# Sample state and memory rows loaded early into other buffers, their products spread over the inversion, half of the memory values' product inside cross attention

## Chip, cores and metric

One core of one Trainium2 chip. The time is that of one execution of the whole program on the device, in microseconds (us).

## What is computed

One decoder layer for a prompt of 256 tokens and 8 sample tokens that share the weights (model width 1024, 264 tokens in all):

```
x += W_out [ ConformerConv(group A) | GatedDeltaNet(group B) ](RMSNorm(x) @ W_in)
x += CrossAttn(RMSNorm(x), memory K/V)
x += MoE_top4of32_clampedSwiGLU(RMSNorm(x))
then a final RMSNorm

prompt, delta rule in chunks:  t_inv = (I + lower)^-1;  u = t_inv @ v_beta;  w = t_inv @ (k_beta * exp(gc))
                               v_new = u - w @ s;  o = (q * exp(g)) @ s + a @ v_new;  s = s * exp(g_last) + k' @ v_new
sample, delta rule in one step: s = s * exp(g);  v = (v - s.k) * beta;  s = s + k v^T;  o = s.q
memory:                        m = RMSNorm(mem);  mk = m @ w_mk;  mv = m @ w_mv      (prompt; kept as outputs)
cross attention:               softmax(q k^T / 16) v, with mk, mv for the prompt, a cache of K and V for each sample
```

The new states, the memory keys and values and the last rows ahead of both convolutions are outputs too. The state of the samples is 8 x 4 matrices of 128x128 (2 MB), each sample's cached keys and values are 256 x 1024 (1 MB each).

## The kernel before

The program has two parts. The second is the expert loop: 32 experts, whose weights (six pieces of 2 MB each) SP streams into eight slots, each piece being requested when TensorE has used the one before it in its slot. The first part, about 400 us, is everything up to the routing, and it is what the change touches.

In the first part TensorE's work is a list of jobs, `pre_moe_jobs`. Job n writes PSUM bank n modulo 8. It waits until job n-8 has been drained (copied out by VectorE or ScalarE), and for its operands. The list alone sets TensorE's order. VectorE and ScalarE each have an order of their own: over the inversion they walk through the same list and take what is theirs, after it their order is written out by hand. SP issues the loads of weights, states and caches in one written order, with waits for the release of each buffer; a wait there holds everything behind it. GpSimd issues the stores in the same way, and the broadcast of the sample queries.

The jobs that the text speaks of, in the order of the list before:

- `qkv`, `z`, `glu_b`, `glu_a`: projections (line L549), 3.6 us each. VectorE runs the short convolution on qkv, ScalarE its nonlinearity.
- The inversion, seven levels by doubling, two chunks: `inv_t` transposes (L698), `inv_x` multiplies (L705, copied by ScalarE), `inv_d` multiplies (L713, merged by VectorE at L1689). Between them stand fills, `glu_b` and `glu_a` in levels 1 to 4, `v_tok`, `k_tok` and `qk` in level 5, `z` 3 in level 6.
- `w_neg` (L722), `v_new` (L734), `state` (L744), `o_t` (L754): the products of the two chunks, each of which needs the copy of the one before it.
- `tail_g` (L850) and `tail_c` (L858): transposes for the rows kept as outputs; `s_decay`, `s_kq`, `s_krow`: small products for the samples.
- `s_read` (L782): each sample's state times its key and query; `s_rd` (L793) picks its diagonal blocks, `s_vrow` transposes the new values, and `s_outer` (L801) makes the outer products that VectorE adds into the state (L1741).
- `mem_t` (L809): transposes of the memory rows, copied by ScalarE; `mk`, `mv` (L819): memory keys and values, four jobs of 7 us each; `mk_t` (L829).
- `ln_mean`, `ln_var` (L569): need the whole wide convolution. That is 140 steps on VectorE (`conv_some`, L1628 to L1643, mostly L1630), done a few at a time between other work and the rest after `s_outer`.
- `w_out`, `q_s` (L885), `x_norm`, `xq`: to the queries. The sample queries go through memory and come back broadcast (`q_bc`, L519); VectorE multiplies them with each sample's cached keys (L1782), which frees the key's buffer (`k_used`).
- `s_score_t` (L925), `score` (L897), `prob_t` (L906), `s_prob_t`, `s_attn` (L945: cached values, freed by `v_used`), `attn` (L918), `s_attn_t`, `xo`, and the routing.

The buffers that matter: `ring` has twelve slots of 1 MB. Its first eight hold the weights (a group of 512 columns takes two), the last four (`scratch`) hold the inversion's tiles and the sample state, later cached keys and values. `region_m` holds the prompt's tiles, later the memory's. `region_p` holds the projections, later queries and probabilities. The loads around the change are on SP:

```
if g >= 4:
    wait_filled(sp, *LAST[g - 4])
sp.dma_start(wslot(g), cols(w, c0)).then_inc(sem(f"group{g % 4}"), 16)
if g == 8:
    wait_drained(sp, "inv_d", LEVELS - 1, 1)
    sp.dma_start(s_state, st_gdn[0].rearrange("b h k v -> k (b h) v")).then_inc(sem("s_state_in"), 16)
    wait_drained(sp, "state", 1)
    wait_drained(sp, "o_t", 1)
    sp.dma_start(mem_tok, mem_prompt[0].rearrange("(t p) d -> p t d", p=P)).then_inc(sem("mem_in"), 16)
```

## Time and profile before

| what | value |
|---|---|
| median of three runs | 1346.7 us (1345.5 to 1347.29) |
| the profiled execution | 1345.48 us, its span 1343.4 us |
| mean granted TensorE clock | 0.988 |
| TensorE (PE) busy | 1297.1 us, 97% |
| VectorE (DVE) busy | 456.9 us, 34% |
| ScalarE (ACT) busy | 222.4 us, 17% |
| GpSimd (POOL) busy | 28.8 us, 2% |
| bytes moved | 469.98 MB, mean 350 GB/s |
| expert loop | from 400.10 us on |

The shares are means over parts that differ: the expert loop takes 70% of the span and has TensorE and the DMA engines busy all the time. A line of the timeline gives start, duration, engine, line of the kernel, operation, tiles and count; idle time of the engine ahead of it stands in brackets with what ended it. A float32 matmul shows as two records.

### The profile page before, as it was taken

How to read it: one execution, taken by the hardware profiler on the slowest of the kernel's cores; microseconds unless marked ns; L12 is line 12 of the kernel's file. 1: busy time of each engine (PE TensorE's matmuls, PEld its weight loads, DVE VectorE, ACT ScalarE, POOL GpSimd, SP SyncE). 2: the span in 40 equal slices, each digit the busy share in tenths (PEclk: the TensorE clock that was granted, in tenths of full speed). 3: DMA queues.
4: the chain of work that ended last, by engine and by line, in shares of the span. 5: the costliest groups of instructions: out<-in, count | busy, mean ns of one | idle time of the engine just before them, and what ended most of it. 6: DMA issues, size and time to landing. Idle time of an engine off the chain costs nothing.

```text
span 1343.4 us, 17566 instructions
## 1 busy us (share of the span) xinstructions
PE 1297.1 (97%) x6598; PEld 610.5 (45%) x6598; DVE 456.9 (34%) x1324; ACT 222.4 (17%) x454; POOL 28.8 (2%) x73
## 2 busy tenths in 40 slices
PE   9999779998999999999999999999999999999996
PEld 6878754686663333333333333333333333333333
DVE  4655739218332222322223322223322223322224
ACT  3241132321131001101001101001110001110002
POOL 3000010000000000000000000000000000000000
PEclk9999889998999999999999999999999999999998
DMA  9310166498867999999999999999999999999992
GB/s 310 143 64 0 56 239 213 162 349 342 312 279 304 425 428 428 428 429 428 428 429 428 429 428 428 429 428 429 429 427 429 429 429 428 428 429 428 429 428 83
DMA packets 56651, 469.98 MB, mean 350 GB/s; under 512 B 6852, under 2 KB 7077, under 8 KB 32029
## 3 DMA queue, kind: packets, MB, share of 16 engines
q1 hardware_dynamic: 50538, 457.34, 82.1%
q0 software_dynamic: 3264, 11.40, 2.5%
q10 hardware_dynamic: 2819, 0.83, 0.3%
q8 instruction: 20, 0.33, 0.1%
q14 instruction: 10, 0.08, 0.0%
HBM read 463.84 MB, written 6.29 MB: 350 GB/s over the span
## 4 chain that ended last, share of the span: by engine, by line
PE 86%; DMA 7%; DVE 4%; ACT 1%; issue 1%; DVEq 0%; SPq 0%; POOL 0%; POOLq 0%; ACTq 0%
PE bank L1006 53%; PE bank L549 10%; PE bank L1052 5%; DMA ring<-in_w_gu 5%; PE bank L819 4%; PE bank L1019 3%; PE bank L1038 2%; PE bank L1032 1%; DMA region_p<-q_scratch 1%; PE bank L705 1%; PE bank L897 1%; PE bank L713 1%; PE bank L625 1%; DVE ring L1782 1%; PE bank L945 1%
## 5 line engine op out<-in xcount | busy, mean ns | idle before, releaser
L1006 PE MATMUL bank<-ring,region_p 128*64 128x512 f32 x2304 | 503.1, 594 | 1.7 <-DMA ring<-in_w_gu 1.0
L1006 PEld LDWEIGHTS bank<-ring,region_p 128*64 128x64 f32 x2304 | 163.0, 137 | 325.7 <-issue 321.8
L1937 DVE TENSOR_SCALAR region_p<-bank 128x512 f32<-128x512 f32 x32 | 22.1, 692 | 613.4 <-PE bank L1038 613.4
L1006 PE MATMUL bank<-region_m,region_p 128*64 128x512 f32 x768 | 169.5, 594 | 0.5 <-DMA region_m<-in_w_gu 0.5
L549 PE MATMUL bank<-hT,ring 128*128 128x264 f32 x512 | 119.6, 391 | 0.0
L1914 DVE TENSOR_TENSOR xT<-xT,bank 128x264 f32<-128x264 f32 x264 | 95.3, 423 | 60.7 <-PE bank L1052 60.7
L549 PEld LDWEIGHTS bank<-hT,ring 128*128 128x128 f32 x512 | 96.5, 192 | 16.1 <-issue 0.4
L1006 PEld LDWEIGHTS bank<-region_m,region_p 128*64 128x64 f32 x768 | 54.3, 137 | 108.7 <-issue 107.3
L1006 PE MATMUL bank<-region_p 128*64 128x512 f32 (+1 forms) x396 | 97.1, 608 | 0.1
L1393 ACT COPY region_p<-bank 128x264 f32<-128x264 f32 x33 | 12.5, 378 | 473.4 <-PE bank L1032 473.4
L1052 PE MATMUL bank<-region_p 64*128 64x264 f32 x528 | 81.0, 415 | 0.5 <-ACT region_p L1393 0.5
L1415 ACT COPY region_p<-bank 128x512 f32<-128x512 f32 x32 | 18.7, 585 | 244.8 <-PE bank L1006 244.8
L1052 PEld LDWEIGHTS bank<-region_p 64*128 64x128 f32 x528 | 49.5, 186 | 15.9 <-DVE xT L1914 5.9
L819 PE MATMUL bank<-ring,region_m 128*128 128x512 f32 x128 | 56.0, 594 | 0.3 <-DVE ring L1741 0.3
L1630 DVE SCALAR_TENSOR_TENSOR region_p<-region_p,par 128x256 f32<-128x256 f32 x120 | 48.3, 476 | 0.0
L1019 PEld LDWEIGHTS bank<-ident,region_p 128*128 128x128 f32 x260 | 27.2, 141 | 38.6 <-DVE region_p L1945 26.0
L1006 PEld LDWEIGHTS bank<-region_p 128*64 128x64 f32 (+1 forms) x396 | 22.4, 134 | 47.3 <-issue 45.6
L1019 PE MATMUL bank<-ident,region_p 128*128 128x128 f32 x260 | 42.6, 287 | 0.7 <-ACT region_p L1397 0.7
L819 PEld LDWEIGHTS bank<-ring,region_m 128*128 128x128 f32 x128 | 24.1, 190 | 29.4 <-issue 27.8
L1038 PE MATMUL bank<-region_p 32*64 32x512 f32 x384 | 35.2, 613 | 0.0
L1945 DVE TENSOR_TENSOR region_p<-region_p 128x512 f32<-128x512 f32 x32 | 33.6, 1051 | 1.1
L1397 ACT COPY region_p<-bank 128x512 f32<-128x512 f32 x33 | 19.3, 585 | 65.9 <-PE bank L1006 65.9
(378 smaller groups left out, 903.1 us busy)
## 6 DMA issues: line engine op xcount, KB each, us to landing
ring<-in_w_gu SPq DMA_DIRECT2D x96, 2048.0 KB, 20.7
ring<-in_w_dn SPq DMA_DIRECT2D x48, 2048.0 KB, 24.7
region_m<-in_w_gu SPq DMA_DIRECT2D x32, 2048.0 KB, 22.1
region_m<-in_w_dn SPq DMA_DIRECT2D x16, 2048.0 KB, 26.1
ring<-in_w_in SPq DMA_DIRECT2D x6, 2048.0 KB, 15.6
ring<-in_cache_mem_k SPq DMA_DIRECT2D x6, 1024.0 KB, 15.3
ring<-in_cache_mem_v SPq DMA_DIRECT2D x6, 1024.0 KB, 9.8
ring<-in_w_mk SPq DMA_DIRECT2D x2, 2048.0 KB, 8.4
```

The source lines that it names most:

```text
L549: m = pe.matmul(ps(key)[:, 0:width], w[:, k, f * P:(f + 1) * P], src[:, k, 0:width], start=(k == 0), stop=(k == KT - 1))
L819: ins = pe.matmul(ps(key)[:, :], memT[:, k, t * P:(t + 1) * P], wslot(g)[:, k, :], start=(k == 0), stop=(k == KT - 1))
L1006: ins = pe.matmul(bank[n][u * SLOTS:(u + 1) * SLOTS, :], lhs, rhs, start=start, stop=stop)
L1019: ins = pe.transpose(bank[dst_bank][:, c * P:(c + 1) * P], n[:, c * P:(c + 1) * P], ident[:, :])
L1038: ins = pe.matmul(bank[n][u * SLOTS:(u + 1) * SLOTS, :], one_hot[r * E:(r + 1) * E, :], bias_sb[r * E:(r + 1) * E, u * 512:(u + 1) * 512], ...
L1052: pe.matmul(bank[SCATTER_BANKS[n % 4]][:, 0:T], y_rows[u * SLOTS:(u + 1) * SLOTS, c * P:(c + 1) * P], scat[u * SLOTS:(u + 1) * SLOTS, :], ...
L1397: act.copy(hg_rows, bank[2][:, :]).then_inc(sem("hg_rows_ready"), 1)
L1415: act.copy(y_rows, bank[5][:, :]).then_inc(sem("y_ready"), 1)
L1630: ins = dve.scalar_tensor_tensor(out=conv[:, f, 0:TP], in0=src, scalar=dw(j, f), in1=conv[:, f, 0:TP], op0=ALU.mult, op1=ALU.add)
L1914: dve.tensor_tensor(xT[:, d, :], xT[:, d, :], bank[SCATTER_BANKS[n % 4]][:, 0:T], ALU.add).then_inc(sem("scat_added"), 1)
L1937: dve.tensor_scalar(xg, bank[0][:, :], 7.0, None, ALU.min).then_inc(sem("glu_clipped"), 1)
L1945: dve.tensor_tensor(act_rows.rearrange("p (v q) -> p q v", v=4), xl.rearrange("p (q v) -> p q v", v=4), sg.rearrange("p (q v) -> p q v", v ...
```

## The change

The list of jobs is written anew. `tail_g` moves up between the projections. `v_tok`, `qk` and `k_tok` become fills of levels 1 to 4, `z` 3 and the small sample jobs fills of level 5, `s_read` a fill of level 6. The memory's transposes stand between the state products. `s_outer` follows directly on `mk` 0. `mv` 0 and 1 stand beside `ln_mean` and `ln_var`, `mv` 2 and 3 go behind `score` in cross attention, on both sides of `s_score_t`. The attn jobs are split around both halves of `s_attn`.

The sample state is loaded in two halves, into `region_p` (free after the short convolution) and into `scratch` (free after `qk`), the memory rows into `region_p` after `k_tok`. All three loads stand on SP ahead of group 7. The weights of `mv` 2 and 3 become group 13, behind those of `w_out` and `xq`. Cached keys and values have five buffers instead of six. VectorE's convolution steps are spread anew over the levels: 81 of 140 stand ahead of `s_outer` instead of 78. ScalarE waits for the state's store ahead of the copies of `xq`. GpSimd's store of the memory values moves behind the broadcasts. VectorE takes the sample scores after the prompt's, and sums `s_attn_t` by four reductions instead of sixteen small operations.

```
-    fill = [[(n, i)] for i in range(4) for n in ("glu_b", "glu_a")]
-    fill += [[("v_tok", 0), ("v_tok", 1), ("k_tok", 0), ("k_tok", 1)], [("qk", 0), ("qk", 1)], [("z", 3)]]
+    turned = [[], [("v_tok", 0), ("v_tok", 1)], [("qk", 0), ("qk", 1)], [("k_tok", 0)], [("k_tok", 1)], [], []]
+    solved = [[]] + [[("glu_b", i)] for i in range(4)] + [[("z", 3)], [("s_read", 0), ("s_read", 1)]]
+    merged = [[]] + [[("glu_a", i)] for i in range(4)] + [[("tail_c",), ("s_krow",), ("s_decay",), ("s_kq",)]]
...
+    jobs += [("mem_t", 6), ("mem_t", 7), ("mk", 0)]
     jobs += [("s_outer", g) for g in range(sample_groups)]
-    jobs += [("mk", 2), ("mk", 3)]
...
+    jobs += [("mv", 2), ("s_score_t",), ("mv", 3)]
...
-        jobs += [("s_prob_t",)] if t == 0 else [("s_attn", 0)]
-    jobs += [("attn", d) for d in range(8)] + [("s_attn", 1), ("s_attn_t",)]
+    jobs += [("s_prob_t",)] + [("attn", d) for d in range(4)] + [("s_attn", 0), ("attn", 4), ("attn", 5)]
+    jobs += [("s_attn", 1), ("attn", 6), ("attn", 7), ("s_attn_t",)]
...
-        s_state = carve(scratch, 0, BH * P, "p (c n) -> p c n", c=BH)
+        s_state = [carve(base, 0, BH * P // 2, "p (c n) -> p c n", c=BH // 2) for base in (region_p, scratch)]
...
-              for v in [ring[:, 8 + i, :] for i in range(4)] + [region_m[:, 0:2048], region_m[:, 4096:6144]]]
+              for v in [ring[:, 8 + i, :] for i in range(4)] + [region_m[:, 4096:6144]]]
...
+                if g == 7:
+                    for j in range(3):
+                        wait_filled(sp, "tail_g", j)
+                    sp.wait_ge(sem("qkv_conv"), QF)
+                    half = st_gdn[0].rearrange("(m b) h k v -> m k (b h) v", m=2)
+                    sp.dma_start(s_state[0], half[0]).then_inc(sem("s_state_in"), 16)
+                    for c in range(NT):
+                        wait_drained(sp, "qk", c)
+                    sp.dma_start(s_state[1], half[1]).then_inc(sem("s_state_in"), 16)
+                    wait_drained(sp, "k_tok", 1)
+                    sp.dma_start(mem_tok, mem_prompt[0].rearrange("(t p) d -> p t d", p=P)).then_inc(sem("mem_in"), 16)
                 if g >= 4:
                     wait_filled(sp, *LAST[g - 4])
                 sp.dma_start(wslot(g), cols(w, c0)).then_inc(sem(f"group{g % 4}"), 16)
...
-                        conv_some(10)
+                        conv_some({2: 10, 3: 10, 4: 13, 5: 13}[lv])
...
-                        conv_some(6)
+                        conv_some(7)
...
+            act.wait_ge(sem("s_state_out"), 32)
```

**TensorE, levels 5 and 6 and the state products.** Before, from the fifth inv_x on (`ring 128x128` is inv_x, the first L549 z 3):

```order
L705 MATMUL bank<-ring 128x128 x8
L678 MATMUL bank<-ident,region_p 128x128 x16
L713 MATMUL bank<-region_m,ring 128x128 x8
L688 MATMUL bank<-region_p 128x128 x8
L698 MATMUL bank<-ident,region_m 128x128 x8
L705 MATMUL bank<-ring 128x128 x8
L549 MATMUL bank<-hT,ring 128x264 x8
L713 MATMUL bank<-region_m,ring 128x128 x8
L722 MATMUL bank<-region_m 128x128 x4
```

The same place now (L710 is inv_x, L718 inv_d, L864 tail_c, L703 inv_t, L787 s_read, L798 s_rd, L727 w_neg):

```order
L710 MATMUL bank<-ring 128x128 x8
L554 MATMUL bank<-hT,ring 128x264 x8
L718 MATMUL bank<-region_m,ring 128x128 x8
L864 MATMUL bank<-ident,region_p 38x128 x4
L776 MATMUL bank<-ident,rn 128x128
L767 MATMUL bank<-small,ones 128x64
L771 MATMUL bank<-small,ones 128x32
L703 MATMUL bank<-ident,region_m 128x128 x8
L710 MATMUL bank<-ring 128x128 x8
L787 MATMUL bank<-region_p,rn 32x512 x4
L787 MATMUL bank<-ring,rn 32x512 x4
L718 MATMUL bank<-region_m,ring 128x128 x8
```

The sixteen transposes of v_tok and k_tok (L678) and qk (L688) are gone from level 5, and s_read stands where z 3 stood.

**TensorE in cross attention.** Before (L925 is s_score_t, L897 score, L906 prob_t, L931 s_prob_t, L945 s_attn, L918 attn):

```order
L925 MATMUL bank<-ident,s_sc 32x128 x2
L897 MATMUL bank<-region_m,region_p 128x256 x16
L906 MATMUL bank<-ident,region_p 128x128 x8
L931 MATMUL bank<-ident,mix 128x32 x2
L906 MATMUL bank<-ident,region_p 128x128 x8
L945 MATMUL bank<-ring,mix 32x512 x8
L945 MATMUL bank<-region_m,mix 32x512 x8
L918 MATMUL bank<-region_p,region_m 128x256 x16
L945 MATMUL bank<-ring,mix 32x512 x16
```

Now (L824 is mv):

```order
L903 MATMUL bank<-region_m,region_p 128x256 x16
L824 MATMUL bank<-ring,region_m 128x512 x8
L931 MATMUL bank<-ident,s_sc 32x128 x2
L824 MATMUL bank<-ring,region_m 128x512 x8
L912 MATMUL bank<-ident,region_p 128x128 x16
L937 MATMUL bank<-ident,mix 128x32 x2
L924 MATMUL bank<-region_p,region_m 128x256 x8
L951 MATMUL bank<-ring,mix 32x512 x4
L951 MATMUL bank<-region_m,mix 32x512 x4
L951 MATMUL bank<-ring,mix 32x512 x8
L924 MATMUL bank<-region_p,region_m 128x256 x4
L951 MATMUL bank<-ring,mix 32x512 x8
```

The prompt's scores come first, two mv jobs stand behind them, and four matmuls (two attn jobs) remain between the halves of s_attn instead of sixteen.

## Rows read from the trace of the kernel before

**Rows 1.** The page, span in 40 slices of 33.6 us, tenths: granted clock, DMA share

```profile
PEclk9999889998999999999999999999999999999998
DMA  9310166498867999999999999999999999999992
```

**Rows 2.** Windows of 20 us: busy us (and instructions) per engine, clock, DMA share, GB/s

```profile
140.00:160.00 20.00, 15.06 (x99) 13.88 (x98) 17.62 (x39) 2.34 (x4) 0.00 (x0) 0.83 0.00 1
...
180.00:200.00 20.00, 16.30 (x68) 8.98 (x69) 5.40 (x17) 7.76 (x17) 1.01 (x2) 0.76 0.53 195
...
220.00:240.00 20.00, 18.82 (x56) 9.35 (x55) 20.00 (x52) 6.32 (x13) 0.72 (x1) 1.00 0.76 240
...
320.00:340.00 20.00, 13.20 (x60) 9.93 (x64) 12.85 (x66) 7.70 (x22) 0.00 (x0) 0.83 0.63 252
```

**Rows 3.** Timeline of TensorE, inversion to s_read: start, us, idle before in brackets

```profile
92.57 3.73 PE L549 MATMUL bank<-hT,ring 128*128 128x264 f32 x16
...
102.95 2.02 PE L705 MATMUL bank<-ring 128*128 128x128 f32 x16 [0.44 <-DVE ring L1683]
...
148.45 1.25 PE L698 MATMUL bank<-ident,region_m 128*128 128x128 f32 x8 [1.43 <-DVE region_m L1689]
153.21 3.76 PE L705 MATMUL bank<-ring 128*128 128x128 f32 x16 [3.51 <-DVE ring L1683]
156.76 4.68 PE L549 MATMUL bank<-hT,ring 128*128 128x264 f32 x16
...
164.25 1.13 PE L722 MATMUL bank<-region_m 128*128 128x128 f32 x8 [1.02 <-DVE region_m L1689]
...
183.69 3.64 PE L782 MATMUL bank<-ring,rn 128*32 128x512 f32 x16 [6.45 <-issue]
```

**Rows 4.** Timeline of TensorE: first mk job, ln_mean, w_out

```profile
191.80 7.11 PE L819 MATMUL bank<-ring,region_m 128*128 128x512 f32 x16
...
240.67 1.95 PE L569 MATMUL bank<-region_p,ones 128*128 128x264 f32 x8
...
257.97 28.64 PE L549 MATMUL bank<-mix,ring 128*128 128x264 f32 x128
```

**Rows 5.** DMA: us from issue to landing; cache loads (L392); the second q_bc

```profile
ring<-in_state_gdn SPq DMA_DIRECT2D x1, 0.5 KB, 19.5
```

```profile
DMA to landing us min/median/max: 6.4/10.6/20.4
```

```profile
304.98 8.02 DMA region_p<-q_scratch
```

**Rows 6.** Timeline of TensorE in cross attention, and the expert loop's first matmuls

```profile
324.43 0.59 PE L925 MATMUL bank<-ident,s_sc 128*32 128x128 f32 x2 [4.86 <-DVE s_sc L1782]
324.88 9.36 PE L897 MATMUL bank<-region_m,region_p 128*128 128x256 f32 x32
336.09 1.35 PE L906 MATMUL bank<-ident,region_p 128*128 128x128 f32 x8 [1.86 <-DVE region_p L1808]
...
342.89 7.17 PE L918 MATMUL bank<-region_p,region_m 128*128 128x256 f32 x32
349.99 3.64 PE L945 MATMUL bank<-ring,mix 128*32 128x512 f32 x32
...
400.10 2.94 PE L1006 MATMUL bank<-region_p 128*64 128x512 f32 x12
```

**Rows 7.** Timeline of VectorE: inv_t copies, s_outer to the convolution's end

```profile
152.38 1.28 DVE L1683 COPY ring<-bank 128x512 f32<-128x512 f32 x2
...
206.98 8.36 DVE L1741 SCALAR_TENSOR_TENSOR ring<-ring,small,bank 128x128 f32<-128x128 f32 x32 [3.06 <-PE bank L801]
215.26 21.46 DVE L1630 SCALAR_TENSOR_TENSOR region_p<-region_p,par 128x256 f32<-128x256 f32 x54
...
238.80 1.32 DVE L1748 SCALAR_TENSOR_TENSOR mix<-mix,par 128x1056 f32<-128x1056 f32 x1
```

More of the change, by code:

```diff
@@ L24, in pre_moe_jobs @@
         jobs += [("qkv", f), ("x_t", f - 1)]
-    jobs += [("qkv", f) for f in range(9, 12)]
-    jobs += [("z", 0), ("decay_small",)]
+        if f == 6:
+            jobs += [("tail_g", 0)]
+    jobs += [("qkv", 9), ("qkv", 10), ("tail_g", 1), ("qkv", 11)]
+    jobs += [("z", 0), ("tail_g", 2), ("decay_small",)]
     jobs += [("decay_row", 0), ("decay_row", 1), ("beta_row", 0), ("beta_row", 1)]
@@ L33, in pre_moe_jobs @@
     for lv in range(1, levels):
-        jobs += [("inv_x", lv, 0), ("inv_x", lv, 1)]
-        jobs += fill.pop(0)
-        jobs += [("inv_d", lv, 0), ("inv_d", lv, 1)]
+        jobs += turned[lv] + [("inv_x", lv, 0), ("inv_x", lv, 1)]
+        jobs += solved[lv] + [("inv_d", lv, 0), ("inv_d", lv, 1)]
         if lv < levels - 1:
-            jobs += fill.pop(0)
-            jobs += [("inv_t", lv, 0), ("inv_t", lv, 1)]
-    for f in fill:
-        jobs += f
-    jobs += [("w_neg",), ("v_new", 0), ("state", 0), ("v_new", 1), ("o_t", 0), ("o_t", 1), ("state", 1)]
@@ L43, in pre_moe_jobs @@
-    jobs += [("tail_g", j) for j in range(3)] + [("tail_c",)]
-    jobs += [("s_decay",), ("s_kq",), ("s_krow",), ("s_read", 0), ("s_read", 1)] + [("mem_t", c) for c in range(8)]
-    jobs += [("s_rd",), ("mk", 0), ("s_vrow",), ("mk", 1)]
+            jobs += merged[lv] + [("inv_t", lv, 0), ("inv_t", lv, 1)]
+    jobs += [("s_rd",), ("w_neg",), ("v_new", 0), ("mem_t", 0), ("mem_t", 1), ("state", 0), ("o_t", 0), ("s_vrow",)]
+    jobs += [("mem_t", 2), ("mem_t", 3), ("v_new", 1), ("mem_t", 4), ("mem_t", 5), ("state", 1), ("o_t", 1)]
@@ L46, in pre_moe_jobs @@
+    jobs += [("mem_t", 6), ("mem_t", 7), ("mk", 0)]
     jobs += [("s_outer", g) for g in range(sample_groups)]
-    jobs += [("mk", 2), ("mk", 3)]
-    jobs += [("o_norm", h) for h in range(4)]
-    jobs += [("mv", 0), ("mv", 1)] + [("mk_t", j) for j in range(4)]
-    jobs += [("ln_mean",), ("mv", 2), ("ln_var",), ("mv", 3)]
+    jobs += [("mk", 1), ("mk", 2), ("mk", 3)]
+    jobs += [("o_norm", h) for h in range(4)] + [("mk_t", j) for j in range(4)]
+    jobs += [("ln_mean",), ("mv", 0), ("ln_var",), ("mv", 1)]
@@ L1250, in _ @@
             order = sorted(JOB, key=JOB.get)
-            for key in order[JOB[("inv_t", 0, 0)]:JOB[("w_neg",)]]:
+            for key in order[JOB[("inv_t", 0, 0)]:JOB[("mk", 0)]]:
                 if key[0] == "inv_x":
@@ L1270, in _ @@
-            wait_filled(act, "tail_c")
-            drained(act.copy(tail_rows[0:HC + TS, :], ps(("tail_c",))[0:HC + TS, :]), ("tail_c",))
-            ln_exp_table()
-            wait_filled(act, "s_decay")
-            act.activation(s_eg, ps(("s_decay",))[:, 0:BH], ACT.Exp)
-            drained(act.copy(s_beta, ps(("s_decay",))[:, BH:2 * BH]), ("s_decay",))
-            wait_filled(act, "s_krow")
-            drained(act.copy(k_row, ps(("s_krow",))[:, 0:P]), ("s_krow",))
-            for m in range(2):
-                wait_filled(act, "s_read", m)
-                drained(act.copy(s_prod[m], ps(("s_read", m))[:, :]), ("s_read", m))
@@ L1281, in _ @@
[L1281 to L1283 removed]
+                elif key[0] == "tail_c":
+                    wait_filled(act, "tail_c")
+                    drained(act.copy(tail_rows[0:HC + TS, :], ps(("tail_c",))[0:HC + TS, :]), ("tail_c",))
+                elif key[0] == "s_krow":
+                    wait_filled(act, "s_krow")
+                    drained(act.copy(k_row, ps(("s_krow",))[:, 0:P]), ("s_krow",))
+                elif key[0] == "s_decay":
+                    ln_exp_table()
+                    wait_filled(act, "s_decay")
+                    act.activation(s_eg, ps(("s_decay",))[:, 0:BH], ACT.Exp)
+                    drained(act.copy(s_beta, ps(("s_decay",))[:, BH:2 * BH]), ("s_decay",))
+                elif key[0] == "s_read":
+                    m = key[1]
+                    wait_filled(act, "s_read", m)
+                    drained(act.copy(s_prod[m], ps(("s_read", m))[:, :]), ("s_read", m))
+                elif key[0] == "w_neg":
+                    wait_filled(act, "w_neg")
+                    drained(act.mul(w_neg.rearrange("p h n -> p (h n)"), ps(("w_neg",))[:, :], -1.0), ("w_neg",))
+                elif key[0] == "v_new":
+                    c = key[1]
+                    wait_filled(act, "v_new", c)
+                    drained(act.copy(v_new[c].rearrange("p h n -> p (h n)"), ps(("v_new", c))[:, :]), ("v_new", c))
+                elif key[0] == "mem_t":
+                    c = key[1]
+                    wait_filled(act, "mem_t", c)
+                    drained(act.mul(memT[:, c, :], ps(("mem_t", c))[:, 0:NMEM], pcol("mem", c)), ("mem_t", c))
```

174 lines of the change are left out of this document (86 added, 88 removed).

## The prediction

> **What bounds the kernel now.** I read the page first, then windows of 20 us, then the timelines of TensorE and VectorE, last the DMA rows. The page's slices show a clock under full speed at the start of the span and again between about 134 and 200 us and near 330 us, and DMA engines that hardly work between 80 and 160 us [rows 1]. The windows give the places: the granted clock is 0.83 in 140:160, 0.76 in 180:200 and 0.83 in 320:340, and in those windows TensorE works 15.1, 16.3 and 13.2 of 20 us; elsewhere it is nearly always busy [rows 2]. So TensorE bounds the program, and what can be won ahead of the expert loop is its waits there and the work that it then does at 1.2 GHz (granted clock 0.50) instead of 2.4 GHz.
>
> The timeline of TensorE names them [rows 3]. After the fifth level of the inversion it waits 1.43 and 3.51 us; the next inv_x (L705) then takes 3.76 us where the same sixteen records took 2.02, and z3 (L549) 4.68 where 3.73 is usual: 4.9 us of waits and 2.7 of slow work. Ahead of s_read (L782) it waits 6.45 us, and everything up to the first memory keys' product at 191.80 [rows 4] runs at the lower level: half of 8.1 us is 4.05. The cause is one DMA row: the state rows take 19.5 us from issue to landing, queued behind weights [rows 5]. In cross attention it waits 4.86 us for VectorE's sample scores and 1.86 for probabilities, and the prompt scores (L897) take 9.36 us, where a product of the same form (L918) takes 7.17 [rows 6].
>
> The expert loop begins at 400.10 [rows 6] and is not touched. Its first eight pieces are loaded ahead of it, each further one is released by its use, so I let it move as a block: what TensorE gains or loses before it, the end gains or loses.
>
> **The change, part by part.** All is counted against the profiled execution, 1345.48 us, whose span is 1343.4; it lies 1.2 us below the median of the three runs, 1346.7.
>
> 1. State rows early. The loads move ahead of group 7 on SP's queue, to a time when DMA is idle. The wait of 6.45 and the slow 4.05 go: -10.5. What is new behind SP's waits: group 7 stands behind qk and k_tok, but it must wait for z3 anyway, and z3 now comes at level 5, after both. Its first user is mk 2, over 30 us later. So nothing.
>
> 2. The inversion's fills. v_tok, qk and k_tok leave level 5 for levels 1 to 4, where VectorE has spare time. At the turn of level 5 it still does 7 steps of the convolution (21.46 us for 54, so 0.40 each [rows 7]: 2.8) and a copy of inv_t (1.28 for two [rows 7]) before TensorE goes on; against that stand the new fills tail_c, s_krow, s_decay and s_kq. I put the wait at 2.9 in place of 4.9, and since it lies between waits that lost the clock (3.51) and those that did not (1.02), I charge half of the 2.7, 1.3. Together -7.6 + 4.2 = -3.4, with bounds -6 and -1.
>
> 3. tail_g goes ahead of the inversion. Its matmuls cost the same in either place; one of its copies now stands on ScalarE's path to the lengths: +0.6. The small waits of 0.4 to 1 us around the state products [rows 3] get mem_t as a fill and new ones come with s_rd: 0, with bounds of 1 on either side.
>
> The first mk job thus starts at 191.8 - 10.5 - 3.4 + 0.6 = 178.5.
>
> 4. VectorE becomes the bound at ln_mean. s_outer now follows mk 0 (7.0 us) directly, so VectorE can begin it at 178.5 + 7.0 + 0.2 = 185.7. From s_outer's start to the end of the convolution it needs now 238.80 - 206.98 = 31.8 us without a gap [rows 7]; 59 steps are left then instead of 62, so 1.2 less. The convolution ends at 216.3. TensorE meanwhile has s_outer, mk 1 to 3 (21), o_norm with its wait and mk_t: 27.8 us from 185.5, thus it is there at 213.3 and waits 3.1. That is close to the 3.51 that was followed by slow work, and a longer wait never kept the clock in this trace; I charge 2.5 (after the three waits 2.7, 4.05 and 2.2 were lost). From ln_mean to the first w_out are two sums and two mv jobs, as now: 257.97 - 240.67 = 17.3 [rows 4]. w_out starts at 216.4 + 17.3 + 2.5 = 236.2, which is 21.8 earlier; 13.8 of this is only the work of mv 2 and 3, moved out.
>
> 5. Cross attention. From w_out to the loop are now 142.1 us. The waits of 4.86 and 1.86 and the slow 2.2 go (-8.9), since mv 2 and mv 3, 6.9 to 7.1 each [rows 4], stand there as cover: +13.9. After the sample keys VectorE needs some 10 us (scores, exponentials, probabilities) and has the prompt scores, mv 2, s_score_t and mv 3, 21 us, to do it in, less what the keys come late. That cover bears it: xo's second half is now issued ahead of the key loads 5 to 7 on SP's queue, and even 4 us more on the keys would end inside it. With that cover gone the old 6.7 come back. SP's key loads as a whole start behind w_out 3 (14 us later than now, relative to w_out), but VectorE begins on them 44 us after w_out's start, when q_bc has landed, so this too costs nothing. ScalarE's new wait for the state's store and GpSimd's later store of the memory values have 60 and 10 us to spare.
>
> 6. A new wait at s_attn 1. With five buffers in place of six, three value loads (5, 6, 7) instead of two wait for s_attn 0, and only two attn jobs (7.17 for eight [rows 6], so 1.8) stand between the halves instead of eight. s_attn takes 3.64 for four samples [rows 6], 0.9 each. If s_attn 0 starts at 0, value load 7 is issued at 2.7, and TensorE wants it at 3.6 + 1.8 + 2.7 = 8.1. The cache loads of this trace land 6.4 to 20.4 us after issue, median 10.6 [rows 5]; at 6.4 it lands at 9.1 (wait 1.1), at 10.6 at 13.3 (wait 5.2). The queue is empty at that moment but three loads go together, so I take 4.0, and 1.0 for the clock behind it. The Trainium skill (DMA: Bandwidth & Descriptors, Measured, HBM to SBUF) gives 6.15 us for 1 MB; an estimate by that figure has a wait of 0.8 and the end 3.2 us earlier than with my 4.0. The shortest cache load of this trace, 6.4, stands close to it, the median does not.
>
> Back half: -8.9 + 13.9 + 5.0 = +10.0. **Sum: 1345.48 - 21.8 + 10.0 = 1333.7.**
>
> **Rivals.** (a) Shorter: the clock holds at all three new waits (-1.3, -2.5, -1.0) and the value load lands at once (-2.9): 1326.0. For it: each new wait is at most 4 us, against 3.5 to 6.5 now. Against it: 3.51 did not keep the clock. (b) Longer: the keys and values queue. q_bc's second round takes 8.02 us now with little beside it [rows 5], and xo's 2 MB will be in flight with it; then value load 7 at 5.2, all clocks lost (+1.3, +0.7) and 2.5 more where sample probabilities or the level-5 turn come late: 1339.4. (c) The early load does not take effect, because a wait ahead of it on SP or the buffer's release holds it until the end of the inversion; then 10.5 comes back, 1344.2. Against it: its waits are all met by level 2. (d) Slower than before: VectorE's convolution is what sets w_out, and it ends where it ends now, at 238.8 instead of 216.3. VectorE works 20.00 of 20 us in 220:240 [rows 2], and its total work does not shrink, so if its idle time before s_outer is not what TensorE's waits made it but its own late chains (s_rd's eight small steps now stand ahead of the copy of state 0), the moved mv jobs are paid in the back while nothing comes off in front: +22.5, 1356.2. This decides from a convolution's end later than 229 on (13 us over mine); slower by what can be told is from 232. Against it: its pieces fit when they are added up, and 81 of the 140 steps stand ahead of s_outer, where 78 do now.
>
> **How the numbers follow.** A measurement of this kernel can tell about 0.2%, 2.7 us, from no change. My forecast, 1333.7 with its own bounds 1330 to 1337.5, gets 0.57; (a) 0.20, (b) 0.16, (c) 0.03, (d) 0.04. Forecast, (a) and (b) are all faster: 0.93; (c) counts as same, 0.03; (d) as slower, 0.04. The range reaches from a little under (a) to a little over (b), 1324 to 1341, and leaves out (c), (d) and the tails of (a) and (b), under 2 in 10.
>
> **What would show it.** Right: no wait ahead of s_read; first mk job near 178.5; VectorE without a gap from s_outer to about 216; a wait of some 3 us at ln_mean, with granted clock 0.5 behind it; w_out near 236; no wait between the last xq and prob_t; a wait of 1 to 5 us inside s_attn 1; the loop's start near 388.3, and from there to the end the same 943.3 us as now. Wrong: a wait for the state rows, a convolution's end past 220, waits at prob_t, or a loop that does not keep its length because its DMA stream, which works all the time there [rows 1], did not move with TensorE.

## The result, and the profile after

The changed kernel takes 1329.79 us (median of four runs, 1329.64 to 1332.12) against 1346.99 us for the kernel before in runs beside it (1345.5 to 1350.29): a ratio of 0.9873, 95% interval 0.9852 to 0.9894. It is faster by about 17 us; 1333.7 was forecast, with a range of 1324 to 1341. The profiled execution took 1329.92 us, its span 1327.9 us, at a mean granted clock of 0.992.

The page, span in 40 slices of 33.2 us. Against [rows 1] the granted clock of the first half no longer has a slice under 9, and DMA moves more data in the slices that held 0 and 1:

```profile
PEclk9999999999999999999999999999999999999998
DMA  9421624797949999999999999999999999999991
```

Windows of 20 us, columns as in [rows 2]. The clock is under 1.00 in 140:160, 200:220 and 320:340:

```profile
140.00:160.00 20.00, 17.36 (x113) 13.71 (x112) 18.53 (x45) 5.73 (x12) 0.00 (x0) 0.91 0.57 204
...
200.00:220.00 20.00, 15.03 (x51) 9.24 (x50) 15.85 (x41) 7.78 (x15) 0.71 (x1) 0.91 0.67 235
...
320.00:340.00 20.00, 17.04 (x95) 7.62 (x94) 4.91 (x14) 0.58 (x1) 2.03 (x4) 0.91 0.87 349
```

The timeline of TensorE from the inversion to the first w_out (answers to [rows 3, 4]; L693 is the line of qk and of kk, a product of the same form ahead of the inversion, and kk at 84.77; L710 inv_x, L787 s_read, L749 state, L824 mk and mv, L574 ln_mean and ln_var, L554 here w_out):

```profile
84.77 2.02 PE L693 MATMUL bank<-region_p 128*128 128x128 f32 x16 [1.34 <-DVE region_p L1606]
...
142.60 2.02 PE L710 MATMUL bank<-ring 128*128 128x128 f32 x16 [0.44 <-DVE ring L1700]
...
154.32 2.96 PE L710 MATMUL bank<-ring 128*128 128x128 f32 x16 [2.20 <-DVE ring L1700]
157.21 1.73 PE L787 MATMUL bank<-region_p,rn 128*32 128x512 f32 x8
...
166.07 1.13 PE L749 MATMUL bank<-region_m 128*128 128x128 f32 x8 [0.29 <-issue]
...
174.34 7.03 PE L824 MATMUL bank<-ring,region_m 128*128 128x512 f32 x16
...
213.24 3.70 PE L574 MATMUL bank<-region_p,ones 128*128 128x264 f32 x8 [3.79 <-DVE region_p L1659]
...
232.29 28.64 PE L554 MATMUL bank<-mix,ring 128*128 128x264 f32 x128
```

s_read has no wait; [rows 3] had 6.45 us there. Level 5 of the inversion keeps one wait, 2.20 us in place of 1.43 and 3.51, and inv_x and half of s_read behind it still run in part at the lower level (2.96 and 1.73 us where 2.02 and 1.06 are seen at full clock). The first mk job comes at 174.34 and not at 191.80 [rows 4], w_out at 232.29 and not at 257.97. VectorE has taken the bound at ln_mean. Its timeline from the s_outer products (L1762) to the end of the convolution, which [rows 7] had at 238.80:

```profile
182.46 4.22 DVE L1762 SCALAR_TENSOR_TENSOR region_p<-region_p,small,bank 128x128 f32<-128x128 f32 x16 [4.50 <-PE bank L806]
...
213.08 1.32 DVE L1770 SCALAR_TENSOR_TENSOR mix<-mix,par 128x1056 f32<-128x1056 f32 x1
```

It is idle for 4.50 us ahead of s_outer, and then TensorE waits 3.79 us for it 31 us later. The end of cross attention and the loop's start (answers to [rows 6]; L912 prob_t, L924 attn, L951 s_attn, L988 position, L1012 the loop):

```profile
307.72 7.03 PE L824 MATMUL bank<-ring,region_m 128*128 128x512 f32 x16
314.59 1.91 PE L912 MATMUL bank<-ident,region_p 128*128 128x128 f32 x16
...
329.65 1.06 PE L951 MATMUL bank<-region_m,mix 128*32 128x512 f32 x8 [1.48 <-DMA region_m<-in_cache_mem_v]
332.20 1.52 PE L951 MATMUL bank<-ring,mix 128*32 128x512 f32 x8 [1.48 <-DMA ring<-in_cache_mem_v]
333.64 3.18 PE L924 MATMUL bank<-region_p,region_m 128*128 128x256 f32 x8
340.54 28.64 PE L554 MATMUL bank<-region_p,ring 128*128 128x264 f32 x128
376.48 0.38 PE L988 MATMUL bank<-region_p,tri_strict 128*128 128x32 f32 x2 [1.04 <-DVE region_p L1889]
382.77 2.94 PE L1012 MATMUL bank<-region_p 128*64 128x512 f32 x12 [0.16 <-DVE region_p L1927]
```

prob_t follows mv 3 without a wait, where [rows 6] had 4.86 and 1.86 us. New are two waits of 1.48 us for value loads inside s_attn. The cache loads' time to landing (answers to [rows 5]) was:

```profile
DMA to landing us min/median/max: 5.2/12.7/18.0
```

Of the 17.3 us by which the loop starts earlier (400.10 to 382.77), its block gives 1.8 back, 1.4 of it in its first products, which took 15.37 us where the kernel before had 13.95 for the same 64 records. The gaps ahead of them, 0.69 and 0.76 us, are the same in both; the granted clock was 0.66 in 388:392 in this execution, and 1.00 at the same place before.

### The profile page after: what moved, and what is told of

The parts are those of the page before. It is cut to its first block, busy times and chain, and to the rows that moved or that the text cites. A ratio compares the mean times of both kernels' runs of the same rounds, so it can differ in the third digit from the quotient of the medians.

```text
span 1327.9 us, 17561 instructions
## 1 busy us (share of the span) xinstructions
PE 1294.5 (97%) x6598; PEld 607.0 (46%) x6598; DVE 456.2 (34%) x1313; ACT 221.7 (17%) x454; POOL 30.1 (2%) x74
## 3 DMA queue, kind: packets, MB, share of 16 engines
HBM read 463.84 MB, written 6.29 MB: 354 GB/s over the span
## 4 chain that ended last, share of the span: by engine, by line
PE 87%; DMA 6%; DVE 4%; ACT 1%; issue 1%; DVEq 0%; SPq 0%; POOL 0%; POOLq 0%; ACTq 0%
PE bank L1012 53%; PE bank L554 12%; PE bank L1058 5%; DMA ring<-in_w_gu 5%; PE bank L1025 3%; PE bank L824 3%; PE bank L1044 2%; DVE region_p L1646 2%; PE bank L1038 1%; PE bank L710 1%; PE bank L718 1%; DMA ring<-in_cache_mem_v 1%; PE bank L630 1%; PE bank L903 1%; PE bank L924 1%
## 5 line engine op out<-in xcount | busy, mean ns | idle before, releaser
L1012 PE MATMUL bank<-ring,region_p 128*64 128x512 f32 x2304 | 504.5, 595 | 2.0 <-DMA ring<-in_w_gu 1.3
L1012 PEld LDWEIGHTS bank<-ring,region_p 128*64 128x64 f32 x2304 | 162.9, 137 | 327.5 <-issue 323.3
L1012 PE MATMUL bank<-region_m,region_p 128*64 128x512 f32 x768 | 169.5, 593 | 0.5 <-DMA region_m<-in_w_gu 0.5
L554 PE MATMUL bank<-hT,ring 128*128 128x264 f32 x512 | 118.7, 388 | 0.0
L1012 PEld LDWEIGHTS bank<-region_m,region_p 128*64 128x64 f32 x768 | 54.3, 137 | 108.7 <-issue 107.3
L554 PEld LDWEIGHTS bank<-hT,ring 128*128 128x128 f32 x512 | 95.5, 190 | 15.8 <-issue 0.4
L1012 PE MATMUL bank<-region_p 128*64 128x512 f32 (+1 forms) x396 | 97.1, 607 | 0.2 <-DVE region_p L1927 0.2
L824 PE MATMUL bank<-ring,region_m 128*128 128x512 f32 x128 | 56.0, 593 | 0.3 <-DVE region_p L1762 0.3
L1012 PEld LDWEIGHTS bank<-region_p 128*64 128x64 f32 (+1 forms) x396 | 22.4, 134 | 47.3 <-issue 45.6
L824 PEld LDWEIGHTS bank<-ring,region_m 128*128 128x128 f32 x128 | 24.1, 191 | 29.2 <-issue 27.5
## 6 DMA issues: line engine op xcount, KB each, us to landing
ring<-in_w_in SPq DMA_DIRECT2D x6, 2048.0 KB, 15.4
```

Source lines behind the costliest of these rows:

```text
L554: m = pe.matmul(ps(key)[:, 0:width], w[:, k, f * P:(f + 1) * P], src[:, k, 0:width], start=(k == 0), stop=(k == KT - 1))
L824: ins = pe.matmul(ps(key)[:, :], memT[:, k, t * P:(t + 1) * P], wslot(g)[:, k, :], start=(k == 0), stop=(k == KT - 1))
L1012: ins = pe.matmul(bank[n][u * SLOTS:(u + 1) * SLOTS, :], lhs, rhs, start=start, stop=stop)
```

## The experiments

Single executions of one kernel lie 2 to 9 us apart here, so I read each experiment twice: by its ratio to the kernel before, run beside it, and by six stretches of its profiled execution, cut at the kk product ahead of the inversion (1), the first mk job (2), the first w_out (3), the first xo (4) and the loop's first product (5); the first one begins and the last one ends with the span. Two of the four mv jobs (13.8 us) stand in stretch 2-3 in the kernel before and in 3-4 in the changed one. Runs whose names begin with the same letter were taken together on one chip.

```
run                 start-1   1-2    2-3     3-4    4-5   5-end   median us  ratio to before (95%)
before                83.61 108.19  66.17   99.84  42.29  943.3   1346.99
changed               84.77  89.57  57.95  108.25  42.23  945.1   1329.79  0.9873 [0.9852, 0.9894]
x1_state_late         90.14 103.47  59.05  106.30  42.30  943.2   1345.04  0.9973 [0.9957, 0.9988]
x2_fills_in_level5    89.97  94.63  57.98  106.34  43.70  945.1   1339.84  0.9932 [0.9910, 0.9954]
x3_mv_in_front        89.78  87.98  65.99  100.01  42.31  943.3   1331.16  0.9867 [0.9837, 0.9898]
x4_mem_t_behind       89.83  90.52  58.84  106.43  43.70  945.5   1334.29  0.9888 [0.9866, 0.9910]
y0_changed_again      85.04  89.57  57.98  106.35  43.69  945.8   1328.85  0.9850 [0.9826, 0.9873]
y1_clock_held         84.92  87.97  56.29  109.28  45.24  945.6   1331.20  0.9878 [0.9845, 0.9911]
y2_conv_19            85.52  89.36  52.25  106.57  43.69  945.2   1327.25  0.9852 [0.9829, 0.9875]
y3_s_attn_apart       88.97  87.98  57.68  103.36  45.28  944.2   1328.90  0.9858 [0.9835, 0.9882]
z1_conv_and_attn      89.73  89.59  52.25  104.46  43.65  945.2   1323.28  0.9824 [0.9797, 0.9850]
z2_with_inv_fill      88.33  87.97  52.24  103.29  45.29  943.3   1321.38  0.9810 [0.9790, 0.9831]
z3_with_gate_fill     85.07  87.97  52.24  103.84  42.72  944.4   1320.21  0.9815 [0.9792, 0.9837]
z4_both_fills         85.20  87.97  52.24  104.17  42.66  945.7   1318.95  0.9797 [0.9778, 0.9817]
```

The first column already teaches something: among the thirteen rows below the first the start varies by 5 us, though TensorE's jobs up to there are the same. All four profiles of x1 to x4 have a late start, which their medians may hold too; so their stretches say more than their medians set against the 1329.8 us, which was measured apart from them.

**x1: the state rows loaded late.** The changed kernel, with both loads behind the fifth level's copies:

```
-   (both s_state loads ahead of group 7)
+                if g == 9:
+                    ...
+                    wait_drained(sp, "inv_t", LEVELS - 2, 1)
+                    sp.dma_start(s_state[0], half[0]).then_inc(sem("s_state_in"), 16)
+                    sp.dma_start(s_state[1], half[1]).then_inc(sem("s_state_in"), 16)
```

> The changed kernel with one edit: both halves of the sample state are loaded behind groups 7 and 8 and behind the last inv_t of level 5, as late as s_read in level 6 allows. Theory A (every wait of TensorE ahead of s_outer goes through to the end, with the slow work behind it): s_read waits 8 to 12 us, 2 to 4 us of slow work follow, and the end comes 10 to 15 us later than the 1329.8 of the changed kernel: 1340 to 1345. Rival B (VectorE bounds the stretch up to ln_mean, so its 3.8 us of waiting there absorb part): the wait at ln_mean vanishes and the end is later by 4 us less than the wait at s_read, 1334 to 1338. If A holds, the wait at ln_mean stays near 3.8, since VectorE itself waits for s_outer.

TensorE's timeline of this run at level 5 and s_read:

```profile
159.70 3.61 PE L710 MATMUL bank<-ring 128*128 128x128 f32 x16 [2.20 <-DVE ring L1700]
174.45 1.94 PE L787 MATMUL bank<-region_p,rn 128*32 128x512 f32 x8 [11.14 <-issue]
```

SP's timeline of this run:

```profile
160.29 0.87 SPq L419 DMA_DIRECT2D region_p<-in_state_gdn  x1
161.61 5.42 SPq L420 DMA_DIRECT2D ring<-in_state_gdn  x1
```

A wait of 11.14 us is back; stretch 1-2 is 13.9 us longer than in the changed kernel and no wait behind it absorbed that (ln_mean's stays 3.78; 3-4 is 1.95 shorter because s_attn kept its clock, as in x4 and y0 without this edit). So this one load carries most of the gain, and it goes through to the end: with all the other edits in place and only the load late, the median is 1345.04 us against 1348.76 for the kernel before on the same chip, and 13.9 and 10.8 us above x3 and x4 there.

The 13.9 (0.65 of it is inv_x 6, which stands ahead of the wait and took 3.61 us against 2.96) are a price in the new order of jobs and can't be set against the 10.5 of the old one. It is not the same transfer: the halves are issued at 160.29 and 161.61 and the later one landed 12.7 us after its issue, where the one load before took 19.5 [rows 5]. And s_read stands in level 6 here: TensorE had 3.0 us of work between the first issue and this wait, where the kernel before had 13.2. x1 thus doesn't part the early load from the move of s_read, which the early load allows; no run has the load late and s_read in its old place.

**x2: v_tok, k_tok and qk back into level 5.**

```
-    turned = [[], [("v_tok", 0), ("v_tok", 1)], [("qk", 0), ("qk", 1)], [("k_tok", 0)], [("k_tok", 1)], [], []]
+    turned = [[] for _ in range(7)]
...  (in level 5 v_tok and k_tok ahead of z 3, qk ahead of tail_c)
```

> The changed kernel with v_tok, k_tok and qk as fills of level 5 again, as in the kernel before, everything else as changed. Theory A (they hide waits in levels 1 to 4 and give VectorE room at level 5): the waits of 0.44 at inv_x of levels 2 to 4 come back (+1.3), the waits at the turn of level 5 grow from 2.2 to 5 or more with slow work of 2 to 3 behind them, the end 5 to 8 us later: 1335 to 1338. Rival B (the fills only move, the sum of TensorE's waits stays): within 1 us of 1329.8.

```profile
121.55 2.02 PE L710 MATMUL bank<-ring 128*128 128x128 f32 x16 [0.44 <-DVE ring L1700]
...
161.26 2.44 PE L710 MATMUL bank<-ring 128*128 128x128 f32 x16 [2.17 <-DVE ring L1700]
166.82 1.93 PE L787 MATMUL bank<-region_p,rn 128*32 128x512 f32 x8 [3.12 <-issue]
```

Stretch 1-2 is 5.1 us longer, as theory A has it, but not at the place it names. It is not the turn of level 5 that pays: its wait is 2.17 us with these fills in level 5 and 2.20 with them elsewhere. What they buy is three waits of 0.44 us in levels 2 to 4 (1.3 us), and the buffer of the second state half: it comes free behind qk, and with qk late SP issues that half at 160.56 instead of 106.98; that is 3.12 us of wait and 1.4 us of slow s_read behind it, where the changed kernel had 0.7. What shortened level 5's waits from 4.9 to 2.2 us is thus another part of the change (the spread of the convolution or the sample jobs there); no run tells which.

**x3: all four mv jobs ahead of w_out.**

```
-    jobs += [("o_norm", h) for h in range(4)] + [("mk_t", j) for j in range(4)]
-    jobs += [("ln_mean",), ("mv", 0), ("ln_var",), ("mv", 1)]
+    jobs += [("o_norm", h) for h in range(4)] + [("mv", 0), ("mv", 1)] + [("mk_t", j) for j in range(4)]
+    jobs += [("ln_mean",), ("mv", 2), ("ln_var",), ("mv", 3)]
...
-    jobs += [("mv", 2), ("s_score_t",), ("mv", 3)]
+    jobs += [("s_score_t",)]
...  (the weights of mv 2 and 3 become group 9; ScalarE's copies move with them)
```

> The changed kernel with all four mv jobs ahead of w_out again and their weights loaded there, none in cross attention. Theory A (mv 2 and 3 cover VectorE's sample scores and the probabilities): the wait of 3.8 at ln_mean and its slow 1.8 vanish (-5.6), waits of 4.9 and 1.9 and slow work of 2.2 come back in cross attention (+9), the end 2 to 5 us later: 1332 to 1335. Rival B (the move is worth nothing, since the cover is taken from ln_mean and given to cross attention): within 1 us of 1329.8.

```profile
226.45 1.95 PE L574 MATMUL bank<-region_p,ones 128*128 128x264 f32 x8
...
312.09 0.38 PE L931 MATMUL bank<-ident,s_sc 128*32 128x128 f32 x2
314.11 3.39 PE L912 MATMUL bank<-ident,region_p 128*128 128x128 f32 x16 [1.64 <-DVE region_p L1822]
...
318.88 5.35 PE L924 MATMUL bank<-region_p,region_m 128*128 128x256 f32 x16 [0.56 <-ACT region_p L1375]
```

Stretches 2-3 and 3-4 together take 166.0 us, against 166.2 in the changed kernel and 164.3 in its second profile, and the ratio, 0.9867, lies between the changed kernel's two (0.9873 and 0.9850). So the headline edit, half of the values' product moved into cross attention, shows no gain by itself, as rival B has it: in front it uncovers the 3.79 us at ln_mean and 1.8 of slow work, and in cross attention it covers 2.2 us of waits and 3.1 of slow prob_t and attn. The old wait of 4.86 us doesn't return without it. The rows say why: VectorE is done with the sample keys 66.5 us after w_out's start before and 65.6 after it here, much the same, but with the prompt's scores ahead of it TensorE comes to s_score_t only 68.3 us after w_out's start (312.09). No run has the scores in their old order with everything else as changed.

**x4: the eight mem_t jobs in one block behind the state products.**

```
-    jobs += [("s_rd",), ("w_neg",), ("v_new", 0), ("mem_t", 0), ("mem_t", 1), ("state", 0), ("o_t", 0), ("s_vrow",)]
-    jobs += [("mem_t", 2), ("mem_t", 3), ("v_new", 1), ("mem_t", 4), ("mem_t", 5), ("state", 1), ("o_t", 1)]
-    jobs += [("mem_t", 6), ("mem_t", 7), ("mk", 0)]
+    jobs += [("s_rd",), ("w_neg",), ("v_new", 0), ("state", 0), ("o_t", 0), ("s_vrow",)]
+    jobs += [("v_new", 1), ("state", 1), ("o_t", 1)]
+    jobs += [("mem_t", c) for c in range(8)] + [("mk", 0)]
```

> The changed kernel with the eight mem_t jobs behind the products of both chunks instead of between them. Theory A (they are what hides the small waits around the state products, which I had put at no gain in the sum): waits of 0.5 to 1 us come back at state 0, v_new 1 and state 1, and one of up to 1 us where mem_t waits for its copies: the end 2 to 4 us later, 1332 to 1334. Rival B (these waits are gone because v_new no longer has slow neighbours, or because s_rd and s_vrow changed the order): within 1 us of 1329.8.

```profile
171.11 1.13 PE L749 MATMUL bank<-region_m 128*128 128x128 f32 x8 [0.72 <-issue]
```

Both state products wait 0.72 us in place of 0.29 and 0.28: 0.9 us in all, and stretch 1-2 is longer by that (90.52 against 89.57). The waits that theory A expected at v_new 1 and at mem_t are not there. The median, 1334.29, would fit theory A's 2 to 4 us, but this profile also started 5.1 us late; the rows show 0.9.

**y0: the changed kernel once more, beside the next three.**

> The changed kernel itself, unedited, on the chip of the next three runs, as their base. In the four runs before this one the first projections ran at half clock (granted 0.64 in 10:20, where the changed kernel's first profile has 1.00), which puts some 5 us on each of them. Theory A (this comes from the chip or the run, not from the edits): the changed kernel shows it too on such a chip, and takes 1333 to 1335 there. Rival B (the edits cause it): 1329.8 as before, with granted clock 1.00 in 10:20.

It starts early again, at 85.04 us. But y3, on the same chip, starts at 88.97, and z3 and z4, which contain y3's edit, at 85.07 and 85.20: neither the chip nor that edit decides it. Behind the start it has the same waits as the first profile within 0.02 us up to cross attention, but kept the clock in s_attn and lost it at the gate (the stretch between position and the loop's first product): 7.75 us there against 6.29.

**y1: filling products in the two largest waits left.**

```
-            BUSY = {("gmix",): 3, ("xn_t", 0): 4, ("s_attn_t",): 1, ("xo", 0): 3}
+            BUSY = {("gmix",): 3, ("xn_t", 0): 4, ("inv_x", 6, 0): 2, ("ln_mean",): 4, ("s_attn_t",): 1, ("xo", 0): 3}
```

> The changed kernel with matmuls of ones that nobody reads, two ahead of inv_x of level 6 and four ahead of ln_mean, into the bank that the next job overwrites: 1.7 and 3.4 us in waits of 2.2 and 3.8. Theory A (the slow work behind both waits comes from the waits): L710 of level 6 takes 2.0 instead of 3.0 and L574 1.9 instead of 3.7, the end 2 to 3 us earlier than the unedited kernel of the same chip. Rival B (the clock falls by its own rhythm, or the fill delays the job behind it as much as it saves): within 1 us.

```profile
154.47 2.02 PE L710 MATMUL bank<-ring 128*128 128x128 f32 x16 [0.48 <-DVE ring L1700]
...
211.78 2.05 PE L574 MATMUL bank<-region_p,ones 128*128 128x264 f32 x8 [0.34 <-DVE region_p L1659]
...
328.78 1.94 PE L951 MATMUL bank<-ring,mix 128*32 128x512 f32 x8 [1.49 <-DMA ring<-in_cache_mem_v]
330.65 3.78 PE L924 MATMUL bank<-region_p,region_m 128*128 128x256 f32 x8
```

The fills do their work: the clock stays up at both places, and w_out comes 3.4 us earlier than in y0 (1.6 of it in stretch 1-2, 1.7 in 2-3). That is the price of slow work at these two waits. Then it is gone again: after the same 1.49 us in s_attn the clock falls here and did not in y0 (attn 3.78 against 1.99), and the gate takes 9.30 us. The median, 1331.20 us, is no better than y0's 1328.85. That filling early makes the clock fall later is not shown: one profile of each stands against the other.

**y2: eleven more steps of the convolution ahead of s_outer.**

```
-            conv_some(8)
+            conv_some(19)
             for b in range(NG):
                 wait_filled(dve, "s_outer", b)
```

> The changed kernel with 19 instead of 8 steps of the wide convolution between o_t 1 and s_outer on VectorE, where it waits 4.5 us for TensorE: 11 steps of 0.40. Theory A (VectorE's steps behind s_outer set ln_mean): the wait of 3.8 at ln_mean falls to nothing and its slow 1.8 with it, the end 4.5 to 6 us earlier than the unedited kernel. Rival B (s_outer and mk 1 now wait for the longer piece, or ln_mean waits for something else as well): under 2 us earlier.

```profile
209.83 1.95 PE L574 MATMUL bank<-region_p,ones 128*128 128x264 f32 x8
...
227.13 28.64 PE L554 MATMUL bank<-mix,ring 128*128 128x264 f32 x128
```

VectorE's idle 4.50 us ahead of s_outer takes them in: s_outer begins 8.1 us after the first mk job as it did without them, now without a wait. The wait at ln_mean and the slow work behind it are gone, and stretch 2-3 is 5.7 us shorter than in y0 (52.25 against 57.98), to the hundredth in every later run that has this edit. The median shows only 1.6 of it, with overlapping intervals.

**y3: the halves of s_attn six attn jobs apart.**

```
-    jobs += [("s_prob_t",)] + [("attn", d) for d in range(4)] + [("s_attn", 0), ("attn", 4), ("attn", 5)]
-    jobs += [("s_attn", 1), ("attn", 6), ("attn", 7), ("s_attn_t",)]
+    jobs += [("s_prob_t",)] + [("attn", 0), ("attn", 1), ("s_attn", 0)]
+    jobs += [("attn", d) for d in range(2, 8)] + [("s_attn", 1), ("s_attn_t",)]
...  (VectorE copies all eight attn results ahead of s_attn 1)
```

> The changed kernel with s_attn 0 behind attn 1 and s_attn 1 behind attn 7, so six attn jobs (5.3 us) stand between the halves instead of two. Theory A (s_attn 1 waits for value loads 6 and 7, which need 8.6 us from s_attn 0's release to landing): the two waits of 1.5 and the slow work behind them go, the end 3 to 5 us earlier than the unedited kernel. Rival B (the loop's first pieces are loaded later, since s_attn 1 releases their slots later, and give it back as a DMA wait at the loop's start): under 1 us earlier.

```profile
324.94 5.45 PE L924 MATMUL bank<-region_p,region_m 128*128 128x256 f32 x24
330.31 1.92 PE L951 MATMUL bank<-ring,mix 128*32 128x512 f32 x16
332.05 1.04 PE L951 MATMUL bank<-region_m,mix 128*32 128x512 f32 x8
332.98 1.07 PE L951 MATMUL bank<-ring,mix 128*32 128x512 f32 x8
```

Both waits for value loads are gone and stretch 3-4 is 3.0 us shorter than in y0. The gate gave 1.6 back and the start 3.9, neither touched by the edit, while inv_x 6 kept its clock and gave 1.6. The median, 1328.90, is y0's 1328.85: the gain is in the rows and not in the time.

**z1 to z4: the edits of y2 and y3 together, then with fills.** z2 adds `("inv_x", 6, 0): 2` to BUSY, z3 `("position",): 2`, z4 both.

> The two edits that shortened their stretch in the trace, together: 19 conv operations ahead of s_outer (first mk to w_out took 52.3 us with it, 58.0 us without) and s_attn 0 and 1 four jobs apart from where they stand (first mk of the back half to xo took 35.0 us with it, 38.0 us without). Theory A, each wait goes whole and what follows moves up: both stretches as short as in the two runs alone, 52.3 and 35.0 us, and a median 5.7 + 3.0 = 8.7 us under the changed kernel's, 1320. Theory B, the gain is given back at the gate (the span from the first position product to the first gather was 6.3 us at full clock and 9.3 us where the granted clock fell there): 1323 to 1326.

> As z1_conv_and_attn, and two filling products ahead of inv_x 6. Theory A: the wait of 2.19 us before inv_x 6 is 0.48 us with them, so the fill costs no time by itself and saves only the slow work behind (0.9 to 1.4 us where the clock fell there, nothing where it did not): between 0 and 1.7 us under z1. Theory B, the clock falls later instead, as it did in the run with fills at inv_x 6 and ln_mean (gate 9.3 us): no difference from z1, or above it by up to 1.5 us.

> As z1_conv_and_attn, and two filling products ahead of position, in the idle 1.04 us there. If that idle time is what lets the granted clock fall at the gate: the clock stays at 1.00 from 370 us on, the gate takes 6.3 us and not 7.8 to 9.3, the first products of the loop take 13.95 us and not 15.4 to 15.7, and the median is 1.5 to 4.5 us under z1. If the clock falls for the gaps of 0.69 and 0.76 us behind it, or for none of these: no difference within 1 us, the gate 7.8 or more in the profile.

> As z1_conv_and_attn, with both fills (two products ahead of inv_x 6, two ahead of position). If the two gains add: 0 to 1.7 us under z3 and 1.5 to 6 us under z1. If a clock held early is lost later (rival): same as z1 within 1 us, with a stretch of clock 0.5 somewhere between s_attn and the loop.

z1: 5.7 us go whole in 2-3 as before; of y3's 3.0 a wait of 0.98 us for the last value load returns (0, 0.35 and 0.69 in z2 to z4). The median, 1323.28, is 5.6 us under y0's, on another chip; by the ratios to before (0.9824 and 0.9850) it is 3.5, with overlapping intervals. Either is nearer theory B than the full 8.7. Its gate, in the trace:

```profile
374.41 5.33 PE L603 MATMUL bank<-ones 128*128 128x512 f32 x8
379.68 2.94 PE L1012 MATMUL bank<-region_p 128*64 128x512 f32 x12
```

The same place in z4 (position with its fill ahead, then the filling products that stood there already, then the loop):

```profile
364.31 1.88 PE L603 MATMUL bank<-ones 128*128 128x512 f32 x4
366.04 0.30 PE L988 MATMUL bank<-region_p,tri_strict 128*128 128x32 f32 x2
...
368.39 3.70 PE L603 MATMUL bank<-ones 128*128 128x512 f32 x8
372.24 2.94 PE L1012 MATMUL bank<-region_p 128*64 128x512 f32 x12
```

The filling products in the gate were put there to cover VectorE's routing. At full clock they take 3.70 us and the loop is released by VectorE; at the lower level they take 5.3 to 6.5 and are what the loop waits for. With the fill ahead of position the gate took 6.28 and 6.20 us in z3 and z4, against 7.72 and 9.34 in z1 and z2. One profile each is thin, the more as three profiles without the fill (changed, x1, x3) had 6.29 to 6.36. The medians go the same way, 1323.28, 1321.38, 1320.21, 1318.95, and so does the spread, 9.2 us between z1's runs and 2.3 between z4's; but the intervals of the ratios overlap, even z1's and z4's (0.9797 to 0.9850 and 0.9778 to 0.9817), so that the fills help is likely and not shown. The fill did not settle the loop's own first products: 15.63 us in z4, 13.95 in z3, after the same gaps of 0.69 and 0.76. So that part of z3's expectation holds in one of two.

z4 is the best version found: 1318.95 us, 0.9797 of the kernel before, 7 to 10 us under the changed kernel (0.9850 and 0.9873 in its two comparisons; z4's interval overlaps with neither of theirs).

## Why the prediction was right

The bottleneck, the waits that go and the places of the new ones were as forecast; the total was 3.8 us too high for the profiled execution. One term was mis-sized (3), one reason was false (2) and one holds in part (5). That the total came so near is luck in part: the 3.9 us that came off in front and the 1.6 behind w_out stand against 1.8 in the loop, for which there was no term, and four executions of this same kernel in y0 lie between 1325.89 and 1330.36. By its own steps:

1. **State rows early, -10.5:** no wait is left ahead of s_read, the slow work that followed it is gone, and x1 shows that the load is the cause and that its gain reaches the end. The 10.5 are the price in the old order of jobs; the 13.9 of x1 are the price with s_read in level 6 and another transfer, and don't contradict them.
2. **The inversion's fills, -3.4:** the wait at the turn came out at 2.20 us (2.9 forecast), the slow work at 1.6 (1.3), together 0.4 less. The reason given, that v_tok, qk and k_tok leave level 5, falls with x2, where they are back and the wait is 2.17. What did it stays open.
3. **"The small waits ... 0":** this is the term that was mis-sized. Four waits of 0.44, and 1.02, 0.72 and 0.87 us, 4.4 in all, became 0.44, 0.29 and 0.28. I had set the new fills against new waits and taken nothing; they gave 3.4. x2 and x4 show where 1.3 and 0.9 of that come from; the other 1.2 no run divides. With the 0.4 above and 0.9 that no row divides, stretch 1-2 is 4.7 shorter than forecast; the early shift by tail_g was 1.16 in place of 0.6. So mk came at 174.34 and not 178.5.
4. **VectorE bounds ln_mean:** the convolution ended at 213.1 (216.3 forecast; mk was 4.2 early, but s_outer began 8.1 and not 7.2 us after it), the wait was 3.79 (3.1) and the slow work 1.8 (2.5): the sum, 5.6, is as forecast, and y2 shows that both hang on VectorE's order alone. From mk to w_out 57.95 us, 57.7 forecast.
5. **Attention waits -8.9:** gone, as said. That mv 2 and 3 are what covers them holds only in part: x3 has them in front, and 4.86 and 1.86 come back as 1.64, 0.43 and 0.56. That the order of the scores did the rest is read from x3's rows, and not tested by itself.
6. **s_attn 1, 4.0 and 1.0:** waits of 1.48 and 1.48, slow work of 1.6 (1.52 and 3.18 us for 1.06 and 1.99). The estimate by the figure of the Trainium skill (DMA: Bandwidth & Descriptors, Measured, HBM to SBUF), 6.15 us for 1 MB and so a wait of 0.8, was too short; that figure is the time in which the DMA engines are busy, without the making of descriptors ahead of it, and not the time from issue to landing. Mine, 4.0 and 1.0, was 0.4 too long. The last load needed 8.56 us here, on the row

```profile
323.59 8.56 DMA ring<-in_cache_mem_v
```

which lies between 6.15 and the 10.6 of the median before, and the measurement decides. From w_out to the loop 150.5 us against 152.1 forecast, 0.4 of the difference from s_attn, the rest spread over rows too small to divide.
7. **The loop as a block, 943.3:** it took 945.1. Its DMA stream moved with TensorE, but its first products ran slower by 1.4. I had no term for the clock at the loop's start, since it was at full speed there in the trace before.

The sum: -3.9 at w_out, -1.6 behind it, +1.8 in the loop, 3.7 of the 3.8. Rival (a), 1326.0, expected all clocks to hold, and each of the three new waits was followed by slow work in this execution. (b) met no queue that TensorE waited for: q_bc's loads landed within 8.3 us, and no wait stands between the last xq and prob_t. (c) fell with s_read's missing wait; what it would have cost in the new order, x1 shows. (d) was near in kind, for VectorE did become the bound, but the convolution ended at 213.1 and not past 229; its idle time ahead of s_outer was only 4.50 us, and y2 fills it.

## What to carry to other kernels

Undo an early load alone in the changed kernel to see whether it is the cause, and price it together with the jobs that it lets move up: the wait was 6.45 us with its user in the old place and 11.14 in the new one. When an engine off the critical path becomes the bound, look for its idle time upstream of the wait before moving other work in as cover: eleven steps put into 4.5 idle us shortened the stretch by 5.7, and moving 13.8 us of matmuls showed no gain. Filling products sized for full clock become the wait themselves when the clock falls (3.70 us became 5.3 to 6.5 at the gate). Two fills that held the clock in front brought w_out 3.4 us earlier and left the median where it was: read a fill by the end of the program, not by its own place.
